# A two-block model on one core: the entry's modulation summed in two groups, with the state scan's inputs placed elsewhere

## What is computed

```python
s_c, s_ctx = jax.nn.silu(c), jax.nn.silu(c_ctx)
m = (s_c @ ada_w[l] + ada_b[l]).reshape(-1, 6, 1, D_MODEL)      # mc likewise of s_ctx
h = modulate(x, m[:, 0], m[:, 1])                               # t * (1 + scale) + shift
hc = modulate(xc, mc[0], mc[1])
...
z, xbc, dt_raw, q, f, v, g = _split(t @ w_in, IN_SIZES)         # t is h, then hc
xbc = jax.nn.silu(dwconv1d(xbc, conv_w, conv_b))
...
dt = softplus(dt_raw + dt_bias); a = dt * -exp(a_log)           # into ssd_scan, chunks of 128
```

## Time and profile before

| | |
|---|---|
| median of 3 runs | 2767.06 us (2764.38 to 2767.47) |
| profiled execution | 2763.52 us, of which span 2761.7 |
| mean granted PE clock | 0.978 |
| PE busy | 2595.7 us (94%) |
| DVE / ACT / POOL busy | 1664.4 (60%) / 1112.8 (40%) / 188.0 (7%) |
| moved by DMA | 241.00 MB, mean 87 GB/s |

### The profile page before, as it was taken

How to read it: one execution, slowest core, us unless ns; L and a number is a source line. 1 busy time by engine, 2 the same in 40 slices (tenths; PEclk the granted TensorE clock), 3 DMA queues, 4 the chain that set the end, 5 groups by cost and what they waited for, 6 DMA issues and landing times. The chain is left out here.

```text
span 2761.7 us, 42190 instructions
## 1 busy us (share of the span) xinstructions
PE 2595.7 (94%) x16298; PEld 2035.2 (74%) x16298; DVE 1664.4 (60%) x2633; ACT 1112.8 (40%) x1881; POOL 188.0 (7%) x186
## 2 busy tenths in 40 slices
PE   6978999987989999999999999999899998999998
PEld 3743698865768788887664788878588766888887
DVE  3537512267776688744898798853763676544432
ACT  3433311155663465422534555522322254355521
POOL 0006600013222000000000000000000000000000
PEclk9989999999999999999999999999999999999999
DMA  8734412211114233241121233331431001233232
GB/s 315 242 102 143 149 54 61 68 37 40 40 49 132 61 99 97 77 136 47 48 59 32 69 107 98 91 116 53 129 91 46 3 17 35 88 94 96 84 114 69
DMA packets 382088, 241.00 MB, mean 87 GB/s; under 512 B 7792, under 2 KB 353776, under 8 KB 381936
## 3 DMA queue, kind: packets, MB, share of 16 engines
q1 hardware_dynamic: 381936, 238.89, 28.5%
HBM read 236.24 MB, written 2.10 MB: 86 GB/s over the span
## 5 line engine op out<-in xcount | busy, mean ns | idle before, releaser
L1251 DVE SCALAR_TENSOR_TENSOR ffn_acc<-ffn_pad,cols_sb,ffn_acc 128x512 f32<-128x512 f32 x380 | 263.9, 748 | 32.1 <-ACT ffn_acc L1178 32.1
L249 PE MATMUL bank<-ffn_x_high,pre_high 128*128 128x512 f32 x528 | 207.3, 393 | 5.0 <-DVE ffn_x_low L523 3.7
L250 PE MATMUL bank<-ffn_x_low,pre_high 128*128 128x512 f32 x528 | 205.6, 389 | 0.0
L251 PE MATMUL bank<-ffn_x_high,pre_low 128*128 128x512 f32 x528 | 205.6, 389 | 0.0
L249 PE MATMUL bank<-ffn_x_high,ffn_w_high 128*128 128x512 f32 x528 | 205.5, 389 | 0.0
L250 PE MATMUL bank<-ffn_x_low,ffn_w_high 128*128 128x512 f32 x528 | 205.4, 389 | 0.0
L251 PE MATMUL bank<-ffn_x_high,ffn_w_low 128*128 128x512 f32 x528 | 205.4, 389 | 0.0
L249 PE MATMUL bank<-ffn_h_high,ffn_down_w_high 128*128 128x512 f32 (+1 forms) x546 | 199.6, 365 | 0.8 <-DVE ffn_h_low L1046 0.8
L250 PE MATMUL bank<-ffn_h_low,ffn_down_w_high 128*128 128x512 f32 (+1 forms) x546 | 198.4, 363 | 0.0
L251 PE MATMUL bank<-ffn_h_high,ffn_down_w_low 128*128 128x512 f32 (+1 forms) x546 | 198.4, 363 | 0.0
L811 ACT ACTIVATE ffn_down_w_high<-ffn_down_ring 128x1408 fp32r<-128x1408 f32 (+1 forms) x45 | 60.5, 1344 | 205.2 <-PE bank L251 185.2
(11 more groups left out here) (751 smaller groups left out, 6293.3 us busy)
## 6 DMA issues: line engine op xcount, KB each, us to landing
ada_ring<-in_ada_w SPq DMA_DIRECT2D x48, 1024.0 KB, 7.0
pre_ring<-in_ffn_w_up SPq DMA_DIRECT2D x88, 512.0 KB, 3.7
pre_ring<-in_ffn_w_in SPq DMA_DIRECT2D x44, 512.0 KB, 3.6
ffn_down_ring<-in_ffn_w_down SPq DMA_DIRECT2D x28, 704.0 KB, 4.5
pj_ring<-in_w_in SPq DMA_DIRECT2D x24, 512.0 KB, 3.8
ffn_down_ring<-in_ffn_w_out SPq DMA_DIRECT2D x14, 704.0 KB, 4.2
pre_ring<-in_conf_w SPq DMA_DIRECT2D x18, 512.0 KB, 4.9
gate_ring<-in_mix_w_in SPq DMA_DIRECT2D x32, 256.0 KB, 2.8
```

Source lines behind the costliest of these rows:

```text
L249: pe.matmul(bank, weights[0], acts[0], start=start, stop=False)
L250: pe.matmul(bank, weights[0], acts[1], start=False, stop=False)
L251: return pe.matmul(bank, weights[1], acts[0], start=False, stop=stop)
L1251: dve.scalar_tensor_tensor(out=dst, in0=src, scalar=conv_w(2 * i + j, n), in1=dst, op0=ALU.mult, op1=ALU.add).then_inc(tapped[j], 1)
```

## The change

1. `groups = [[0, 2], [1, 3]]`: the early slabs are summed, turned and biased in two groups of two (new `bias_of`). The feed takes blocks 0 to 3 of x, then 0 to 3 of ctx, then the second half of both (`fed_order`). PE multiplies the first half's items between the first group's turn and the second group's sums (`early`, `as_fed`).
2. Three tiles' split weights are held (`together = 3`), and tile 2's latent products run in the second half; its first four blocks stand alone ahead of that half's feed. The order of the loads follows (`inputs`).
3. Riding slabs: one before the context's second half, one after each turn 1 to 10, the last one in the middle of turn 11.
4. The step widths' products move from `ssd_prepare` into the entry: the latent ones after turn 10, the context's behind the last turn of the modulation.
5. The constants' load becomes SP's work in `ssd_prepare`. `load` and `more_constants` go.
6. In `ssd_prepare` ACT and DVE copy every other transposed job.

```diff
@@ entry
+    groups = [[0, 2], [1, 3]]
+    order = [2 * s + part for group in groups for s in group for part in range(2)]
+    near = DT // 2
+    fed_order = [(who, k) for start in (0, near) for who in range(2) for k in range(start, start + near)]
+    fed_at = {pair: n + 1 for n, pair in enumerate(fed_order)}
+    together = 3
-    behind = {t: [t] for t in range(2, XBC_T - 2)}
-    behind.update({1: [0, 1], XBC_T - 2: [XBC_T - 2, XBC_T - 1]})
...
             def piece(n):
                 if n >= 3:
                     sp.wait_ge(used, n - 2)
-                sp.dma_start(ring[:, n % 3], ada.piece(n)).then_inc(piece_in[n % 3], 16)
+                sp.dma_start(ring[:, n % 3], ada.piece(order[n] if n < len(order) else n)).then_inc(piece_in[n % 3], 16)
...
-            for n in range(3, 2 * EARLY - 2):
-                piece(n)
+            piece(3)
             for t in range(2):
                 slab(t)
-            for n in range(2 * EARLY - 2, 2 * EARLY):
+            inputs(0)
+            for n in range(4, 7):
                 piece(n)
...
+            slab(2)
+            piece(7)
+            inputs(1)
             sp.dma_start(rows[:], ada.sources["rows"]).then_inc(rows_in, 16)
             sp.dma_start(dt_in[:], w_dt).then_inc(steps_in, 16)
             for t in range(XBC_T):
+                if 3 <= t + 2 < XBC_T:
+                    slab(t + 2)
                 for part in range(2):
                     piece(2 * (EARLY + t) + part)
...
+            def early(group, row):
+                for part in range(2):
+                    n = order.index(2 * groups[group][row] + part)
+                    pe.wait_ge(piece_in[n % 3], 16 * (n // 3 + 1))
+                    ada.sums(pe, sums_bank, n % 3, part, row, row == 0 and part == 0, row == 1 and part == 1).then_inc(used, 1)
+            def steps(n):
+                pe.wait_ge(lat_free, XBC_T - 3 + n)
+                for k in range(DT):
+                    three_passes(pe, banks[n][0:2 * SSD_HEADS, 0:SPANS[n][1]], [part[:, k, :] for part in dt_w],
+                                 [part[:, k, :] for part in h[n]], k == 0, k == DT - 1)
+            def as_fed(who, e):
+                for k in range(e * near, (e + 1) * near):
+                    pe.wait_ge(fed, fed_at[who, k])
+                    for t in range(2 if who or e == 0 else together):
+                        product(t, k, who)
...
-            for s in range(EARLY):
-                slab(s, 0, EARLY - 1)
+            for row in range(2):
+                early(0, row)
             pe.wait_ge(const_in, 16)
-            turn(EARLY, 1)
+            turn(len(groups[0]), 1)
             pe.wait_ge(w_low, 2)
...
+            as_fed(0, 0)
+            early(1, 0)
+            as_fed(1, 0)
+            early(1, 1)
+            turn(len(groups[1]), 2)
+            pe.wait_ge(w_low, together)
+            for k in range(near):
+                product(2, k, 0)
+            as_fed(0, 1)
+            slab(EARLY, EARLY, LATE - 1)
+            as_fed(1, 1)
...
+                            if t == XBC_T - 1 and k == near:
+                                slab(LATE - 1, EARLY, LATE - 1)
...
-                for s in behind.get(t, []):
-                    slab(EARLY + s, EARLY, LATE - 1)
-            turn(riders, 2)
+                if t < XBC_T - 1:
+                    slab(EARLY + t, EARLY, LATE - 1)
+                if t == XBC_T - 2:
+                    pe.wait_ge(steps_split, 1)
+                    steps(0)
+            turn(riders, 3)
+            steps(1)
@@ ssd_prepare
+        @block.sync
+        def _(sp):
+            sp.dma_start(consts, source).then_inc(consts_in, 16)
...
-            for n, (start, size) in enumerate(SPANS):
-                for k in range(DT):
-                    mm = three_passes(pe, banks[n][0:heads, 0:size], [part[:, k, :] for part in dt_w],
-                                      [part[:, k, 0:size] for part in h[n]], k == 0, k == DT - 1)
-                mm.then_inc(made, 1)
...
-            for n in range(ahead):
+            for n in range(0, ahead, 2):
                 take(n)
...
+            def take(n):
+                _, _, out, features = jobs[n]
+                dve.wait_ge(turned, n + 1)
+                dve.tensor_copy(out, banks[2 + n % 6][:, 0:len(features) * P]).then_inc(taken_dve, 1)
+
+            take(1)
             dve.wait_ge(steps_turned, 1)
```

More of the change, by code:

```diff
@@ L165, in const @@
         return self.const_sb[:, CONST_AT[name], :] if CONST_AT[name] < ALWAYS else self.some[name]
-    @contextmanager
-    def more_constants(self, names, source):
-        first = CONST_AT[names[0]]
-        with self.room(**{f"const_{names[0]}": [P, len(names), P]}) as (buf,):
-            load(self, [(buf[:], source[:, first:first + len(names), :])])
-            self.some = {name: buf[:, n, :] for n, name in enumerate(names)}
-            yield
     @contextmanager
@@ L1684, in bias, with bias_of @@
         return done
+    def bias_of(self, dve, bank, slabs):
+        per = ADA_W // P
+        turned = bank[:, 0:2 * per * len(slabs)].rearrange("p (t w) -> p t w", w=2)
+        for i, s in enumerate(slabs):
+            tile = s * per
+            at = COL_AT["ada_b0"] + tile
+            raw, add = turned[:, i * per:(i + 1) * per], spread(self.core.cols_sb[:, at:at + per], 2, 2)
+            out = self.mods[0][:, tile:tile + per, :]
+            if tile // DT == 1:
+                done = dve.scalar_tensor_tensor(out=out, in0=raw, scalar=1.0, in1=add, op0=ALU.add, op1=ALU.add)
+            else:
+                done = dve.tensor_tensor(out, raw, add, ALU.add)
+        return done
 class Folds:
@@ L1766, in slab, with inputs @@
                 sp.dma_start(w_ring[:, t % 2], w[:, :, t * P:(t + 1) * P]).then_inc(slab_in[t % 2], 16)
+            def inputs(e):
+                part = slice(e * near, (e + 1) * near)
+                sp.dma_start(x[:, part], ada.sources["x"][:, part]).then_inc(x_in[0][e], 16)
+                sp.dma_start(ctx[:, part], ada.sources["ctx"][:, part]).then_inc(x_in[1][e], 16)
             sp.dma_start(core.cols_sb[:], ada.sources["cols"]).then_inc(cols_in, 16)
@@ L1848, in take_high @@
                 act.wait_ge(slab_in[t % 2], 16 * (t // 2 + 1))
[L1849 to L1851 removed]
+                if t >= together:
+                    act.wait_ge(ctx_done, t - together + 1)
+                act.activation(high[:, t % together], w_ring[:, t % 2], ACT.Copy).then_inc(w_high, 1)
             def silu(t):
@@ L2041, in _ @@
             act.activation(soft[:], soft[:], ACT.Ln, bias=1.0).then_inc(soft_done, 1)
-            for n in range(ahead, later):
+            for n in range(ahead + 1, later, 2):
                 take(n)
@@ L2047, in _ @@
             act.activation(grown[:], here(0), ACT.Exp)
-            for n in range(later, len(jobs)):
+            for n in range(later + 1, len(jobs), 2):
                 take(n)
@@ L2058, in _ @@
                .then_inc(folded, 1)
+            for n in range(ahead, later - 2, 2):
+                take(n)
             dve.wait_ge(soft_done, 1)
@@ L2065, in _ @@
                                      op0=ALU.mult, op1=ALU.mult).then_inc(a_done, 1)
+            take(later - 2)
             dve.wait_ge(summed, 1)
@@ L2069, in _ @@
             dve.tensor_tensor(left[:], total, left[:], ALU.subtract).then_inc(left_done, 1)
+            for n in range(later, later + 4, 2):
+                take(n)
             dve.wait_ge(exp_left, 1)
             dve.tensor_tensor(left[:], left[:], by_way(dt[:]), ALU.mult)
+            for n in range(later + 4, len(jobs), 2):
+                take(n)
 def ssd_scan(core, ada, xbc, x_tok, b_tok, dt, a, a_parts, sides, share, faded, grown, y, nxt):
@@ L3634, in _ @@
                                          op1=ALU.mult).then_inc(normed, 1)
-def load(core, pairs):
-    with core.stage("loaded") as (block, loaded):
-        @block.sync
-        def _(sp):
-            for dst, src in pairs:
-                sp.dma_start(dst, src).then_inc(loaded, 16)
-            sp.wait_ge(loaded, 16 * len(pairs))
 RW_ORDER = [6, 2, 3, 0, 1, 4, 5]
```

109 lines of the change are left out of this document (55 added, 54 removed).

## The result

The changed kernel takes **2750.28 us** (median of 4 runs, 2749.94 to 2750.97) against 2767.26 for the kernel before: a ratio of 0.9934, 95% interval 0.9921 to 0.9946. It is faster by 17 us. A second set of runs on another occasion gave 2749.29 against 2770.94 (0.9928, interval 0.9913 to 0.9944). The forecast was 2740.5 with a range of 2732 to 2748: the sign is right, the gain is smaller than foretold, and the time lies outside the range.

What follows compares the result with a forecast made beforehand. TensorE, busy 94% of the span, was taken as the bound, with stops to remove before the scan. Gains of 9.7 + 0.8 + 3.6 + 11.1 = 25.2 us gave 2738.3 (profile) or 2741.9 (median); forecast 2740.5, range 2732 to 2748.

Steps and rivals of the forecast that it cites:

- part 1: Entry up to turn 3's first product: turn 3 begins at 65.5 instead of 75.15 us, 9.7 us gained.
- the removed stop: Entry's loop, where PE stood 3.49 us for a late piece and then ran slowly: removing it gives 5.4 us.
- squeezed: Rival: first half's products don't fit ahead of piece 7, so part 1 keeps only 5.4 us; 2745, chance 0.06.
- First product: Start of the entry: PE's first product at 25.0 us instead of 36.38.
- Piece 7: Second group's last weights: slot free at 33.0, landed 38.1 after 5.14 us, summed 39.0; feed restarts at 41.1.
- Pieces 12 and 13: Last modulation weights before turn 3: piece 12 lands at 62.0, summed 63.0; piece 13 queues behind, summed 65.5.
- cost nothing: Slab 2's twelve products, at 40.7 to 43.5 us, are free because PE would wait for the feed there.
- Part 2: Turn 3 to the entry's end: tail from turn 10 takes 25.8 instead of 26.6 us, 0.8 us gained.
- Part 3: Constants' load stage between entry and preparation: 4.4 us shrinks to a bare barrier of 0.8, 3.6 us gained.
- Part 4: Preparation before the scan: 23.95 us becomes 12.8 (bounds 11.3 and 15), 11.1 us gained.
- I carry it over unchanged: Everything from the scan on: same code behind a barrier of all engines, so no change in its time.
- relapses of the clock: Rival: clock falls at PE's pauses at the second turn and piece 13; 6 us less gain, 2746, chance 0.12.

Runs made afterwards that it cites:

- three_tiles: one_group with a third tile's split weights held, so DVE takes tile 2's low part ahead of tile 0's taps; 2748.52 us.
- before_again: The kernel before the change, unedited, run once more for a second profile; 2769.23 us.
- act_copies: Changed kernel with all 18 copies of the preparation on ACT again; 2754.16 us.
- steps_back: Changed kernel with the step widths' 48 products in the preparation again; 2754.64 us.
- after_again: The changed kernel, unedited, run once more for a second profile and more times; 2749.29 us.
- bunched: Changed kernel with riding slabs back in pairs after turns 1 and 10, none before the context's second half or in turn 11; 2755.33 us.
- start_delay: Changed kernel behind an added stage in which DVE does five fills of 128x512, delaying everything after it; 2751.73 us.
- fill: Changed kernel with 11 unread matmuls added, 4 ahead of the wait for piece 12 and 7 ahead of piece 13; 2746.72 us.
- load_stage: Changed kernel with the constants' load in a stage of its own again; 2751.35 us.
- one_group: Kernel before with the change's parts 3 to 6, but one group of early sums, old order of feed and loads, two tiles held; 2753.94 us.

## Why the prediction was wrong in size

The step that failed is part 1, and in it the share of the two groups. Of its 9.7 us, 5.4 are the removed stop (so the rival "squeezed" counts it), which leaves 4.3 for the groups. The stop's share came out: three_tiles, with one group, begins turn 3 at 69.58 instead of 75.15, 5.6 us earlier (4.3 against before_again). The groups' share did not: the changed kernel is only 0.7 us ahead of three_tiles in its first profile and 1.4 behind it in its second. With a fourth slot the groups are worth 5.3 us up to turn 3, so it is the late pieces behind three slots that took them. Going by the prediction's own steps:

- **First product** at 25.0: measured 24.83. Copies, chain and arrival of the first group held to 0.2 us.
- **Part 1, 9.7 us**: measured 6.2 in the first pair of profiles, and between the means of two profiles each 4.6 (74.5 and 69.9). The chain was followed rightly, pauses at 7, 11, 12 and 13 included, but three terms in it were too small; together they are the 3.4 us from 65.5 to 68.93. Piece 7: issued at 33.60 instead of 33.0, since the first products ran longer at 1.2 GHz, and 5.4 us on its way instead of 5.14; its sums' copy starts at 40.13, where 41.1 less the chain gives 39.0, and with 0.3 us for x the feed restarts at 42.44 instead of 41.1. By piece 11 this is 1.5 us. Pieces 12 and 13: 13 comes 7.7 us behind 11 (59.36 to 67.07), where 1.5 + 2.6 + 2.6 = 6.7 was taken, 1.0 us. The clock: it fell at piece 13, which the text had as a rival and not in the sum, 0.9 us up to turn 3 and 0.4 in it.
- **The scatter of piece 7.** It came 5.2 to 5.4 us after its issue in the first profile of the changed kernel, act_copies and steps_back, but 6.2 in after_again and bunched and 7.1 to 7.5 in start_delay, fill and load_stage. PE's pause for it grew from 0.3 to 0.5 us to 1.4 and to 2.2 to 2.6 by this. In four of the five late cases (not in bunched) the clock was at 1.2 GHz behind the second turn.
- **"The early half is squeezed"** valued the removed stop at 5.4 us. The number came out, but by luck: one_group shows that the spread riders alone remove the piece's wait and gain nothing, because a wait for tile 2's low part takes its place. It is the third tile that removes this one, and the prediction had taken its products for a mere filler ("cost nothing").
- **Part 2, 0.8**: from turn 3's start to the last silu's end 99.3 us before, 99.26 after (68.93 to 168.19): 0.1. The slow clock at turn 3 lies in this measurement, 0.4 of it; the taps covered the context's step products, as foretold.
- **Part 3, 3.6**: the barriers from the silu's end to ACT's start, 4.4 before and 0.92 after: 3.5; by load_stage 4.3.
- **Part 4, 11.1**: 178.88 to 202.85 before, 169.11 to 181.55 after: 23.97 less 12.44, 11.5. The table load on the path costs 1.28 and the next activation follows within 0.02 us, so no further wait follows a switch here either. That is what the forecast went by; the drain of the Trainium skill (ScalarE: Activation LUTs, What ACT_TABLE_LOAD costs) is not in the trace.
- The sum to the scan was 25.2; in the pair of profiles it is 21.3, on the mean of two each 18.1. Parts 2 to 4 give 15.1 of their 15.5 us in the first pair and 13.5 on the means: in before_again the stop behind turn 10 did not bring the clock down, and in after_again the preparation ran partly at 1.2 GHz.
- **"I carry it over unchanged"** was right for the work and wrong for the time. The first profile of before has 2558.9 us behind the scan, the mean of 14 profiles is 2564.6. Its time, 2763.5, lay under the lowest of the runs shown (2764.38), and a part of the prediction was counted from there: 2740.5 was 1.4 us under the median less 25.2. The median itself was fair (2767 to 2771 in four sets); less the measured 21.3 or 18.1 us it gives 2745.8 or 2749.0, and the kernel took 2750.28 and 2749.29.
- **The range** of 2732 to 2748 gave relapses of the clock 0.12. They occurred in all eight profiles of kernels with two groups and three slots: at piece 13 (the changed kernel, act_copies, steps_back), behind the second group's turn (load_stage, fill, start_delay), at both (after_again), or behind the returned stops (bunched). With a price of 1.3 us and more each they belonged in the likeliest case. The prediction's argument against them, that the present loop's falls had followed pauses of over 3 us, was read from one execution.

## What to carry to other kernels

An earlier start is worth only what the resource behind it can keep up with: here three slots of 1 MB, with 5 to 7.5 us from issue to landing, gave back what two groups had won, and one slot more released it. When a wait is removed, look in the trace for what the same engine would have waited for next: the low part of tile 2 came ready 0.9 us ahead of the late piece, and the profile shows only the last one of two waits. A fall of the clock or a late load in one profile should be looked for in a second one before a sum is built on it. Before a sum is made against one profiled execution, compare its time with those of the other runs; if it lies outside them, the unchanged part of the program must be taken at its usual length.

## What the runs showed of the hardware

- The same code behind the scan took 2558.9 to 2570.7 us, and the longer times go with more time at 1.2 GHz (before 94 us of it and before_again 110 behind the scan; 0.89 and 0.80 in one stretch of 60 us). The clock does not explain all of it.
- The clock fell in some executions and not in others of the same kernel. From 40 to 50 us it was 1.00 in the first profile of the changed kernel (pause of 0.53 us before piece 7) and 0.83 in the second (pause of 1.37). Pauses of 1.0 to 1.3 and 1.5 to 1.6 us before pieces 12 and 13 were followed by sums at 1.2 GHz in four profiles and by sums at 2.4 in two. Nor did a pause of over 3 us settle it: at the stop behind turn 10 the sums took 1.93 us in before (3.10 us of pause) and 1.06 in before_again:

```profile
158.43 1.06 PE L1656 MATMUL bank<-ada_ring,ada_cond 128*32 128x512 f32 x8 [3.12 <-DMA ada_ring<-in_ada_w]
```

- A 1 MB load on a queue that had run empty took 5.2 to 7.5 us from issue to the waiting matmul (33.60 to 38.99 in the changed kernel, 33.73 to 41.20 in load_stage), while in a busy queue the same bytes follow each other at 2.6 us. With a 0.5 MB slab among them the loads from piece 11 to piece 13 took 7.7 us in place of 6.7.
